# Sixteen key and value halves between the score groups, six gate blocks in the values stage, last modulation parts in the second norm: one decoder layer on one core

## What is computed

```python
mod = (silu(c) @ w_ada + b_ada).reshape(B, 1, 9, 1024)          # shift, scale, gate, three times
sh1, sc1, g1, sh2, sc2, g2, sh3, sc3, g3 = [mod[:, :, i] for i in range(9)]
h = rms_norm(x, norm_ffn1) * (1 + sc1) + sh1
x = x + 0.5 * g1 * ((silu(h @ w_gate1) * (h @ w_up1)) @ w_down1)   # 2816 hidden
h = rms_norm(x, norm_mix) * (1 + sc2) + sh2
q_a, k_a, v_a, q_b, k_b, v_b, g_a, g_b = split(h @ w_in)         # 6 x 512, 2 x 1024 columns
q_a, k_a, q_b, k_b = rms_norm of each head of 64
o_a, o_b = attend(...)      # a: MoBA, 8 heads of 64; b: differential attention, 4 heads
y_a, y_b = o_a @ w_branch_moba, rms_norm(o_b) @ w_branch_diff
x = x + g2 * ((sigmoid(g_a) * y_a + sigmoid(g_b) * y_b) @ w_out)
h = rms_norm(x, norm_ffn2) * (1 + sc3) + sh3
x = x + 0.5 * g3 * ((silu(h @ w_gate2) * (h @ w_up2)) @ w_down2)
```

## Time and profile before

| | us |
|---|---|
| median of 3 runs | 829.81 |
| lowest and highest | 829.15, 840.59 |
| the profiled execution: its time | 834.78 |
| its span | 832.6 |
| TensorE busy | 744.2 |
| VectorE busy | 488.8 |
| ScalarE busy | 319.1 |

### The profile page before, as it was taken

The page is one execution under the profiler, slowest core; times in us unless marked ns, Lnnn a source line. Parts: engine busy times, 40 slices in busy tenths (PEclk is TensorE's granted clock), DMA queues, the critical chain, the costliest instruction groups (busy, mean ns, idle before and its releaser), DMA issues. The chain is left out here.

```text
span 832.6 us, 16901 instructions
## 1 busy us (share of the span) xinstructions
PE 744.2 (89%) x6574; PEld 662.2 (80%) x6574; DVE 488.8 (59%) x655; ACT 319.1 (38%) x490; POOL 82.3 (10%) x152
## 2 busy tenths in 40 slices
PE   5589999999997999796886899678897999999997
PEld 2479888899996999685775756238796999999997
DVE  2635544545445898887888565467656545555442
ACT  2434333434333655231211444236335434444341
POOL 0000000000001201242433044410000000000000
PEclk9799999999999899697997999998898999999999
DMA  9978989896666956589999499993452655655530
GB/s 358 371 270 309 324 294 328 294 314 204 243 218 226 372 167 212 167 311 382 381 375 381 172 354 386 387 380 111 147 158 57 196 183 170 196 164 175 185 116 27
DMA packets 132901, 209.51 MB, mean 252 GB/s; under 512 B 6714, under 2 KB 100186, under 8 KB 128738
## 3 DMA queue, kind: packets, MB, share of 16 engines
q1 hardware_dynamic: 121312, 172.05, 60.3%
q0 software_dynamic: 11296, 36.44, 11.7%
q10 hardware_dynamic: 226, 0.10, 0.0%
HBM read 205.31 MB, written 3.24 MB: 250 GB/s over the span
## 5 line engine op out<-in xcount | busy, mean ns | idle before, releaser
L902 DVE TENSOR_TENSOR wlo<-raw,whi 128x1024 fp32r<-128x1024 f32 (+1 forms) x192 | 227.0, 1198 | 203.0 <-ACT whi L623 200.2
L1302 PE MATMUL bank<-hhi,whi 128*128 128x264 f32 x1056 | 310.6, 294 | 20.2 <-DVE hlo L949 10.2
L1303 PE MATMUL bank<-hlo,whi 128*128 128x264 f32 x1056 | 305.4, 289 | 0.0
L1304 PE MATMUL bank<-hhi,wlo 128*128 128x264 f32 x1056 | 304.8, 289 | 0.0
L623 ACT ACTIVATE whi<-raw 128x1024 fp32r<-128x1024 f32 (+1 forms) x192 | 195.2, 1035 | 146.9 <-PE bank L1304 90.0
L1302 PEld LDWEIGHTS bank<-hhi,whi 128*128 128x128 f32 x1056 | 205.5, 195 | 33.5 <-issue 22.0
L1303 PEld LDWEIGHTS bank<-hlo,whi 128*128 128x128 f32 x1056 | 205.4, 194 | 0.1
L1304 PEld LDWEIGHTS bank<-hhi,wlo 128*128 128x128 f32 x1056 | 204.2, 193 | 0.0
L1302 PE MATMUL bank<-ahi,whi 128*128 128x264 f32 x416 | 120.8, 290 | 4.0 <-DVE alo L1274 4.0
L1304 PE MATMUL bank<-ahi,wlo 128*128 128x264 f32 x416 | 119.1, 286 | 0.0
L1303 PE MATMUL bank<-alo,whi 128*128 128x264 f32 x416 | 118.8, 286 | 0.0
(11 more groups left out here) (233 smaller groups left out, 674.3 us busy)
## 6 DMA issues: line engine op xcount, KB each, us to landing
raw<-in_w_ada SPq DMA_DIRECT2D x32, 1024.0 KB, 7.4
raw<-in_ffn_w_gate SPq DMA_DIRECT2D x22, 1024.0 KB, 5.4
raw<-in_ffn_w_up SPq DMA_DIRECT2D x22, 1024.0 KB, 5.5
raw<-in_w_in SPq DMA_DIRECT2D x20, 1024.0 KB, 10.3
raw<-in_ffn_w_down SPq DMA_DIRECT2D x16, 1024.0 KB, 5.4
kvB<-in_cache_k_diff POOLq DMA_DIRECT2D x44, 256.0 KB, 6.8
kvA<-in_cache_k_moba SPq DMA_DIRECT2D x44, 256.0 KB, 7.1
kvA<-in_cache_v_moba SPq DMA_DIRECT2D x44, 256.0 KB, 7.8
```

Source lines behind the costliest of these rows:

```text
L902: dve.tensor_tensor(half_view(wlo[key[1] % 2], key, t), half_view(raw[s], key, t), half_view(whi[key[1] % 2], key, t).bitcast(F32), ALU.su ...
L1302: mm(out, wh, xh, start=start, stop=False)
L1303: mm(out, wh, xl, start=False, stop=False)
L1304: return mm(out, wl, xh, start=False, stop=stop)
```

## The change

Key and value blocks get a common name, W_KV, with eight blocks in the order k0 v0 k1 v1 k2 k3 v2 v3. The projection loop runs over the four query blocks only. All 16 key and value halves stand in rounds u = 0 to 15 of one loop of 18, whose rounds 2 to 17 bring score group u - 2. The norm of a key half is made alone: a sum, a root, a reciprocal and a product of 264 columns. The first key turn stands before the fourth query norm, `own_products` in round 14. No gate block is left in the rounds; blocks 0 and 1 stand in the softmax stage and 2 to 7 in steps 1 to 6 of the values stage. The loads follow: `AHEAD` says behind which use SyncE asks for which block. The ada block 16 goes to the end of the down projection, 17 behind the last row sum.

```diff
-W_QK, W_V, W_GATE, W_BR, W_OUT = 34, 42, 46, 54, 58
+W_QK, W_KV, W_GATE, W_BR, W_OUT = 34, 38, 46, 54, 58
...
+    plan += [("w", W_DN1 + u) for u in range(4)] + ada(ADA_PRO + NPAIR)
+    plan += [("w", W_DN1 + u) for u in range(4, 12)] + [("w", W_QK)] + ada(ADA_PRO + NPAIR + 1) + ada(ADA_PRO + NPAIR + 2)
+    plan += [("w", n) for n in range(W_QK + 1, W_DN2 + 12)]
...
+KV_BLOCKS = [("k", 0), ("v", 0), ("k", 1), ("v", 1), ("k", 2), ("k", 3), ("v", 2), ("v", 3)]
...
-        EXTRA = {0: W_GATE + 7, 2: W_BR, KC - 1: W_BR + 1}
+        AHEAD = {4: [W_KV + 5], 6: [W_KV + 6], 8: [W_KV + 7], 10: [W_GATE], 12: [W_GATE + 1], 14: [W_GATE + 2],
+                 18: [W_GATE + 3, W_GATE + 4], 19: [W_GATE + 5], 21: [W_GATE + 6], 23: [W_GATE + 7], 25: [W_BR]}
+
+        EXTRA = {0: W_GATE + 3, 1: W_GATE + 4, 2: W_GATE + 5, 3: W_GATE + 6, 4: W_GATE + 7, 5: W_BR, KC - 1: W_BR + 1}
...
-            for i in range(4):
-                pool.wait_ge(s_tok, 2 * (i + 1))
-                row_out("k", i // 2, i % 2, ktok, ktoks, s_krow)
             for use in range(KVS, 4 * TS):
                 kv_load(pool, 1, use)
-                if use in (4, 6, 8, 10):
-                    i = (use - 4) // 2
+                if use in K_ROWS:
+                    i = K_ROWS[use]
+                    pool.wait_ge(s_tok, 4 * (i + 1))
+                    row_out("k", i // 2, i % 2, ktok, ktoks, s_krow)
+                if use in V_ROWS:
+                    i = V_ROWS[use]
                     pool.wait_ge(s_vtok, 4 * (i + 1))
                     row_out("v", i // 2, i % 2, vtok, vtoks, s_vrow)
...
+            def k_norm(i):
+
+                v.wait_ge(s_kroot, i + 1)
+                dve.reciprocal(rstd[:, i % 2, :], rstd[:, i % 2, :]).then_inc(s_krecip, 1)
+                v.wait_ge(s_krecip, i + 1)
+                g = 10 + i // 4
+                dve.scalar_tensor_tensor(out=kT[:, i, :], in0=kT[:, i, :], scalar=misc[:, g:g + 1], in1=rstd[:, i % 2, :],
+                                         op0=ALU.mult, op1=ALU.mult).then_inc(s_knorm, 1)
...
+            for u in range(2, 2 * TS + 2):
+                if u - 2 < 16:
+                    kind, i = kv_half(u - 2)
+                    if kind == "k":
+                        k_norm(i)
+                if u % 2 and 5 <= u <= 15:
+                    place_q((u - 1) // 2)
+                if u - 1 < 2 * TS:
+                    turn_keys(u - 1)
+                if u + 3 < 20:
+                    lo(*filler(u + 3))
+                if u == 14:
+                    own_products()
...
-                        if with_ada and u == 7:
-                            ada(4, 0, 16)
...
                 if with_ada:
+                    ada(4, 0, 16)
+                    norm_sum(1, 3)
                     ada(4, 1, 17)
-                    norm_sum(1, 3)
...
+            for u in range(2 * TS + 2):
+                if u < 16:
+                    kv_product(u)
                 if u == 0:
+                    head_sum(3)
+                if 1 <= u < 17:
+                    kind, i = kv_half(u - 1)
+                    if kind == "k":
+                        k_sum(i)
+                    else:
+                        v_turn(u - 1, i)
+                if 3 <= u < 19:
+                    kind, i = kv_half(u - 3)
+                    if kind == "k":
+                        k_turn(i)
+                if u == 2:
+                    replicate_q()
+                    pe.wait_ge(s_nvar, 4)
...
+                if u >= 2:
+                    scores(u - 2)
...
-                gated = 1 <= c <= 2
+                gated = 1 <= c <= 6
...
                     if half == 0 and gated:
-                        gate_half(c + 5, 0)
+                        gate_half(c + 1, 0)
```

More of the change, by code:

```diff
@@ L1027, in down @@
             def down(first, gate, ada):
-                for m in range(3, 27 if ada else 24):
+                for m in range(3, 26 if ada else 24):
                     if ada and m == 4:
@@ L1047, in _ @@
             norm_rows(1)
+            lo(W_QK + 1, 0)
             mod_add(ADAS - 1)
```

332 lines of the change are left out of this document (164 added, 168 removed).

## The result

| | before | after |
|---|---|---|
| device time, median of the runs | 836.15 us (828.55 to 842.70, 20 runs) | 826.5 us (821.55 to 831.24, 20 runs) |
| ratio, 95% interval | 1 | 0.9899 [0.9875, 0.9923] |
| profiled execution, span | 832.6 us | 826.0 us |
| first cache scores (start) | 342.71 | 316.05 |
| reduction behind the scores | 453.43 | 425.98 |

The change makes the kernel 1.0% faster. The ratio is taken between runs made side by side; 829.81 us was the median of the three runs of the kernel before that the forecast started from, so the ratio and not the distance of the medians is the result. The forecast was -15.0 us (-1.8%); the ratio gives -8.4 us of 829.81 and the two profiled spans -6.6.

The account below looks back on a forecast made before the run. The middle was taken as bound by VectorE in query and key projections, with cache reads idle, and by transfers in the cache stages. Terms -28.6, +1.6 and +12.0 summed to -15.0 us: 814.8 against 829.81, range 805 to 828.

Parts of the forecast that it names:

- (a): Down projection: ada block 16 moves to its end, into TensorE's hole during the norm, -1.0 us.
- (b): Projection stage: four key blocks leave, first scores at 314.1 in place of 342.7, -28.6 us including the ada move.
- (c): Score rounds with sixteen key and value halves: VectorE the full engine, 112.3 us against 110.7, +1.6.
- R3: Score stage: transfers recover less, rounds at 7.6 us, whole change -5.6, 824 us; chance 0.08.
- R4: Score stage: TensorE at half clock throughout, rounds at 10.7 us, +44, 874 us; chance 0.06.
- (d): Between scores and values: nothing changes in kind, two gate blocks before the row sum, 0 us.
- (e): Values stage: four more block loads, 10.9 us, and 1.1 for two near paces, +12.0 us.
- R2: Values stage: paced by the chain of steps through the weight split, +20 there, -7 in all, 823 us; chance 0.16.
- R1: Score and values stages: both paces fit without loss, gates at full clock, about -21, 809 us; chance 0.27.
- main case: Whole kernel: the summed forecast of -15.0 us, 811 to 820 us; chance 0.43.

Follow-up runs that it names:

- few loads: Changed kernel with the loads of gate blocks 5, 6, 7 and the first branch block cut to an eighth: values stage 90.0 us, ratio 0.9808.
- three blocks early: Changed kernel with gate block 0 under the last two score rounds, 1 and 2 in softmax, 3 to 7 in values steps 1 to 5: ratio 0.9863.
- the run where it is alone: Changed kernel with four block loads cut to an eighth and VectorE's split and o variance behind the next step's scaling: stage 88.5 us, ratio 0.9823.
- few products, split behind: Changed kernel with gate block 4 to 7 products cut to an eighth, VectorE's split and o variance behind the next step's scaling: 89.1 us, 0.9835.
- both cuts: Changed kernel with gate block 4 to 7 products and four block loads cut to an eighth: values stage 90.8 us, ratio 0.9792.
- split behind: Changed kernel with each split's low half and the o variance moved behind the next step's scaling on VectorE: stage 95.8 us, ratio 0.9914.
- reads first: Changed kernel with gate blocks 5, 6, 7 and the first branch block asked for behind uses 21, 22, 24, 26: stage 100.0 us, ratio 0.9895.
- loads later: Changed kernel with gate blocks 5, 6, 7 and the first branch block each asked for one cache read later: stage 97.2 us, ratio 0.9893.

## Why the forecast was wrong, step by step

**(a)** -1.0: the profiles roughly agree. The first product of W_QK starts at 269.79 ("about 270"), 1.6 us earlier than before (271.42), and alone the part moves the reduction by -0.9. Its measured time alone, -3.5 us with an interval from -1.2 to -5.8, says more than its profile shows; where the rest would be is open.

**(b)** first scores at 314.1: they start at 316.05, 2 us late. VectorE waits 1.62 us for ScalarE's copy at 313.57, a wait that the sum of VectorE's work did not have; the rest is that the third query norm ends 0.5 us later than the sum had it. One mark was missed: I expected no idle DMA stretch at 303 to 308, and there is one (0.02); the keys' buffers are still full there, since the first scores, which free one, start at 316.05.

**(c)** 112.3 for the rounds: from the first scores to the reduction 109.9, so 2.4 below, which pays for (b): VectorE's own sum, 109.3, was right, and of the 3.0 us added for "the two pacing each other" only 0.6 came. VectorE is over 96% busy (I wrote over 95), its wait for landed keys fell from 13.4 to 2.3 (under 5), the clock is 0.93. (b) and (c) together put the reduction 27.45 us earlier, against 27.0 forecast. R3 (rounds at 7.6 us; they are 6.9) and R4 (half clock through the stage) are out.

**(d)** 0: from the reduction to the first transposes 27.3 us before and 27.5 after, by the first table, with the row sum's wait 8.1 where the earlier trace rows had 7.8. Held.

**(e)** +12.0: measured +20.0. This is the step that failed, and in it the sentence "Two paces so near each other cost something" with its +1.1. The 10.9 for the transfers of four blocks was a fair size. But I set the whole stage's transfers, 87 us, against the whole stage's TensorE work, 84, and took the larger. The runs show that the bound changes within the stage (how interval 2 comes to lie so high is read from single profiles, and its scatter is some 3 us):

- Intervals 1 to 3 are held by transfers: 43.8 us in after, 35.1 to 38.4 in the four runs with few loads. The first step uses up its buffers in 10.5 us, while what a step asks for, sixteen pages and one block, 5.24 MB, takes 13.6 us at 386 GB/s. Step 2 pays for it, and the clock falls behind its wait. Ahead of them the DMA engines rest (0.12 from 437 to 450), since no buffer comes free; that this rest is a cause is not shown, for the kernel before rests there too, and three blocks early moved 216 GB/s in it and had a step 2 of 21.2 us.
- Intervals 4 to 7 are held by TensorE, 51.6, and the chain through the split, 52.1 to 52.5; transfers want about 46.5. In interval 4 the chain is another, that through ScalarE's copy of the gate half: 15.5 us of the interval's 16.5 stay when TensorE's products, the loads and the split's place are all taken away.

On this measure my forecast was 88.7 (76.7 and 12.0). Transfers alone would give 43.8 and 46.5, 90.3, which is 1.6 over it. TensorE's 51.6 in place of 46.5 in the second part adds 5.1, and what is left to the 96.7 measured, 1.3, is the coupling. 1.6, 5.1 and 1.3 are the 8.0 that were missing. This is bookkeeping and no proof: the 43.8 is what after itself measured.

TensorE's 84 was also too small, 88.5 in the run where it is alone. The step of 12.1 us in it is a misreading: 491.88 in the earlier trace rows is the start of the last three of six transposes and 504.01 lies among the first; from first to first it is 12.7. And the five steps with gate halves are 68.3 us in that run, 13.7 each: I left out the sixteen 4-column products at L1735 (1.92 us) and the lower clock behind them (1.3 us there, 1.6 in after). The 3.7 us of closing work lie inside the last interval, which the sum already has; this hid part of what was missing.

R2 had the size, "(e) +20, -7", and the sum of the profile is -6.6. Its mechanism is half of the truth: the 13.6 us of transfers per step and the chain through the split are both there, but the chain holds only the second part, beside TensorE; taken out alone it gives 1.0 us. The marks I had named for it did show: transfers at 1.04 only up to about 500, a step of 19.1 beyond "12 to 13.6", a DMA share under 0.9 (0.88 from 515 to 520), and a values stage over 95 us as what would make the whole wrong. Of R1, the terms as listed add up to -21.8 and not -21.

The time fell inside the range (805 to 828). That is no merit of the main case: 826.5, and also 821.4 (0.9899 of 829.81), lie above its 811 to 820, and the upper end of the range was there for R2 and R3.

## What to carry to other kernels

Where a stage is near balance between two engines, cut it into the parts in which each of them has its rest and its crowd, and add up the larger bound of each part; the larger of the two sums over the whole is a floor, not a forecast. Here the larger sum over the whole is 89.1 (few products, split behind), the larger bounds of the parts, 42.6 from that run and 52.5 from both cuts, give 95.1, and 96.7 was measured; the rule was found on this kernel and not tried on another. Look also for a copy that a third engine makes late in its order: in interval 4 no cut of the two large sums changed anything. And when work is taken off such a stage, look at which read stands behind which block on its queue: here asking for the weight blocks one read later, in a version that multiplies a block more ahead of the stage, went with 0.9802 [0.9758, 0.9847] of before against 0.9863 [0.9840, 0.9887], and a stage of 92.7 us against 95.9; by its median it is the fastest version here that computes everything, though the two intervals still touch.

## What the runs showed of the hardware that I had not expected

- A read of four pages of 256 KB that stands behind a 1 MB block on the same queue landed 16.7 us after its issue, while the queues moved 386 to 388 GB/s in all from 460 to 475 us. A block ahead is not needed for a late landing: with few products and few loads, where only 128 KB stood ahead, the read for use 21 took 15.2 us; with few loads alone TensorE waited for no read. The Trainium skill ("DMA: Bandwidth & Descriptors", section "Bandwidth") gives about 358 GB/s for a core when both cores of its memory domain stream, and 425 for one core alone in a transfer of 16 MB; this kernel, on one core, lies between, with 376 GB/s over the 45 us from 455 to 500 and 383 over 30 us in the run with few products and the split behind.
- Behind the sixteen 4-column products at L1735, which have a hole of 0.56 us ahead, the clock fell to its lower level in some kernels and not in others: the granted clock over the next 3 us was 0.52 in after and about that with few loads, with the split behind, with these two together (0.55 from 500 to 503) and with reads first in the changed kernel, and the sixteen value products took 3.0 to 3.6 us. With loads later and in all three versions with three blocks early it stayed at 1.00:

```profile
506.02 1.92 PE L1735 MATMUL bank<-const,om 128*128 128x4 f32 x16 [0.56 <-ACT gT L811]
507.87 1.06 PE L1693 MATMUL bank<-kvA,wpad 128*32 128x512 f32 x8
```

This is loads later, with the same products, the same hole and the same busy time of TensorE ahead (without a break for 5.6 us) as in after, where the second row reads 1.83. In the kernel before, where no hole stands ahead of them, the clock stayed whole as well. The difference is worth 1.6 us, 16.5 against 14.9 for interval 4, in favour of these four versions when their second parts are compared with that of after. What decides between the two is open.
